# Sparse attention's position bias formed inside block 1's first feed-forward product with 128-row one-hots, and a gate unit of 48 columns that stays on the chip

## The reference

```python
gates = jax.nn.sigmoid(g.reshape(bsz, t_len, NSA_HEADS, 3))      # g: the last 48 columns of proj = h @ w_in
def nsa_mixer(q, k_cmp, v_cmp, k_slc, v_slc, k_swa, v_swa, gates, cmp_pos, cmp_w1, cmp_w2, rel_bias):
    kc = compress(k_cmp, 0); vc = compress(v_cmp, 1)              # 15 compressed keys and values
    # head_bias(dist) = tab[t5_bucket(dist)], tab = rel_bias, 32 buckets x 16 heads
    s_c = q @ kc * scale + head_bias(dist_c)                      # compressed branch
    s_s = q @ ks * scale + bias_s                                 # selected branch, the same table
    s_w = q @ kw * scale + head_bias(dist_w)                      # window branch, the same table
    return gb[..., 0:1] * o_c + gb[..., 1:2] * o_s + gb[..., 2:3] * o_w
```

## Time and profile before

| what | value |
|---|---|
| runs, median of 3 | 3845.78 us (3845.76 to 3848.34) |
| profiled execution, span | 3849.2 us |
| TensorE busy with products, weight loads | 97%, 91% of the span |
| VectorE, ScalarE, GpSimd busy | 49%, 15%, 36% |
| mean granted clock of TensorE | 0.986 of 2.4 GHz |
| bias products, gate unit, compression, nv 0 | 2619.71 to 2670.5 us of the span |

### The profile page before, as it was taken

How to read it: one execution, slowest core, us unless ns; L and a number is a source line. 1 busy time by engine, 2 the same in 40 slices (tenths; PEclk the granted TensorE clock), 3 DMA queues, 4 the chain that set the end, 5 groups by cost and what they waited for, 6 DMA issues and landing times.

```text
span 3849.2 us, 67389 instructions
## 1 busy us (share of the span) xinstructions
PE 3729.7 (97%) x29050; PEld 3506.3 (91%) x29050; DVE 1886.3 (49%) x3284; ACT 590.1 (15%) x1321; POOL 1380.1 (36%) x799
## 2 busy tenths in 40 slices
PE   9999999999999999999999999999898999999997
PEld 7888888889989999999999998878696899999997
DVE  2444426572334623111125547471633788888655
ACT  0333311111110111000000000131602211111001
POOL 0000000045546774777760000000350677775000
PEclk9999999999999999999999999999999999999999
DMA  6565665456664553444444554436342344444452
GB/s 258 196 231 211 219 238 189 175 181 225 209 206 173 222 187 144 160 169 176 165 159 162 173 203 164 169 121 171 125 165 109 133 159 172 176 162 162 163 177 84
DMA packets 124442, 677.61 MB, mean 176 GB/s; under 512 B 32208, under 2 KB 38608, under 8 KB 93808
## 3 DMA queue, kind: packets, MB, share of 16 engines
q1 hardware_dynamic: 88784, 584.37, 42.5%
q0 software_dynamic: 11824, 43.00, 3.8%
q10 hardware_dynamic: 23536, 45.92, 3.3%
HBM read 619.99 MB, written 53.25 MB: 175 GB/s over the span
## 4 chain that ended last, share of the span: by engine, by line
PE 91%; DVE 4%; ACT 1%; DVEq 1%; issue 1%; DMA 0%; ACTq 0%; SPq 0%; POOL 0%
PE product_bank L583 56%; PE product_bank L644 25%; PE product_bank L411 2%; PE product_bank L889 1%; PE mixer_bank L1587 0%; PE mixer_bank L1601 0%; PE mixer_bank L1418 0%; DVE arena L1449 0%; PE mixer_bank L800 0%; DVE yT L1446 0%; DVE yT L1161 0%; PE mixer_bank L2644 0%; PE mixer_bank L1410 0%; PE mixer_bank L2678 0%; ACT xT L1116 0%
## 5 line engine op out<-in xcount | busy, mean ns | idle before, releaser
L644 PE MATMUL product_bank<-hT,weight_ring 128*128 128x256 f32 x2752 | 608.6, 380 | 2.5 <-ACT out_stage L683 1.7
L644 PEld LDWEIGHTS product_bank<-hT,weight_ring 128*128 128x128 f32 x2752 | 522.1, 191 | 76.0 <-issue 4.5
L583 PE MATMUL product_bank<-hT,weight_ring 128*128 128x128 f32 x4128 | 518.7, 277 | 12.4 <-DVE out_stage L624 8.4
L583 PEld LDWEIGHTS product_bank<-hT,weight_ring 128*128 128x128 f32 x4128 | 490.0, 193 | 16.8 <-DVE out_stage L624 9.0
L583 PE MATMUL product_bank<-arena,weight_ring 128*128 128x128 f32 x3360 | 419.7, 275 | 1.4 <-DVE hT L624 1.4
L583 PEld LDWEIGHTS product_bank<-arena,weight_ring 128*128 128x128 f32 x3360 | 397.1, 192 | 3.6 <-DVE hT L624 1.6
L618 DVE TENSOR_TENSOR arena<-product_bank,arena 128x128 f32<-128x128 f32 x125 | 36.3, 291 | 640.7 <-PE product_bank L583 639.8
L550 POOL TENSOR_TENSOR arena<-weight_ring 128x1024 f32<-128x1024 f32 x87 | 207.1, 2380 | 353.0 <-PE product_bank L583 277.7
L553 POOL TENSOR_TENSOR weight_ring<-weight_ring 128x1024 f32<-128x1024 f32 (+1 forms) x155 | 331.2, 2137 | 0.0
L3111 DVE SCALAR_TENSOR_TENSOR arena<-arena 128x256 f32<-128x256 f32 x176 | 322.2, 1869 | 14.4 <-ACT arena L3076 11.1
L583 PE MATMUL product_bank<-xT,weight_ring 128*128 128x128 f32 x2144 | 273.9, 277 | 10.4 <-ACT xT L1116 10.4
(11 more groups left out here) (580 smaller groups left out, 5317.4 us busy)
## 6 DMA issues: line engine op xcount, KB each, us to landing
weight_ring<-in_weights SPq DMA_DIRECT2D x212, 2048.0 KB, 8.0
weight_ring<-in_weights SPq DMA_DIRECT2D x132, 512.0 KB, 5.7
weight_ring<-in_weights SPq DMA_DIRECT2D x64, 384.0 KB, 5.7
units<-out_stage ACTq DMA_DIRECT2D x87, 256.0 KB, 7.8
rwkv_keep<-arena ACTq DMA_DIRECT2D x16, 1282.0 KB, 6.1
arena<-units POOLq DMA_DIRECT2D x47, 256.0 KB, 4.5
arena<-rwkv_keep SPq DMA_DIRECT2D x8, 1280.0 KB, 12.0
arena<-units SPq DMA_DIRECT2D x27, 256.0 KB, 8.6
```

Source lines behind the costliest of these rows:

```text
L583: mm = pe.matmul(bank[:, at * P:at * P + P], lhs[:, j, :], rhs[:, j, :], start=g == 0 and n in (0, 3) and j == 0, stop=g == n_groups - 1 a ...
L644: mm = pe.matmul(psg[b][:, half * T:half * T + T], lhs, rhs, start=k == 0, stop=k == 15)
```

## The change

- The bias products move from `nsa_pe` into `ffn_pe`, behind unit 4 of 44 (`BIAS_AT`). VectorE first spreads the table into a block diagonal (`tab_spread`, after its unit 2), so that the 30 products on 32 rows become 8 on 128 rows with 64 columns (the last one 64 rows and 32 columns); the L2637 product stays. VectorE takes them out of PSUM after its unit 5, and adds the compressed mask there.
- The bias rows go to DRAM once (behind GpSimd's unit 8) and are then copied 128 times within DRAM in four parts of 4 heads (768 KB each), behind units 12, 16, 20 and 24.
- The gate unit joins the weave as quarters 57 to 60, with 48 columns instead of 256; ScalarE copies the 48 columns to SBUF, and the store and the load fall away. The sigmoid becomes the first thing after the weave. `beside_mixers` skips every fourth step instead of every third.
- SyncE's `nsa_loads` stands behind nv 1's slot load instead of mem_v 0's, no longer waits for nk before the compression's loads, and takes the queries ahead of nk. The values are loaded where all of it was.
- GpSimd's `nsa_pool` waits for `s5_done` before head 0's tiles instead of before `memT`.
- `n_BC`, `n_rows` and `n_g` lie where the one-hots were, in the constants.

The diff, cut to its core:

```diff
-STORED = ("rkv", "lora", "qk", "v", "gates", "mem_k", "mem_v", "sqk", "sv", "nq", "nkc", "nk", "nv", "ng")
+STORED = ("rkv", "lora", "qk", "v", "gates", "mem_k", "mem_v", "sqk", "sv", "nq", "nkc", "nk", "nv")
...
                 if n == UNIT_AT["branch_b0", 0][0] + RING - 1:
                     gate_loads(sp)
+                if n == UNIT_AT["nv", 1][0]:
+                    nsa_loads(sp)
                 if n == UNIT_AT["mem_v", 0][0]:
-                    nsa_loads(sp)
+                    nsa_value_loads(sp)
...
+        def unit_quarters(pe, name, u, src, step=8, arrives=None, cols=T):
-                        lhs, rhs = src[:, k, half * P:half * P + P], w[:, k, :]
-                    mm = pe.matmul(psg[b][:, half * T:half * T + T], lhs, rhs, start=k == 0, stop=k == 15)
+                        lhs, rhs = src[:, k, half * P:half * P + P], w[:, k, 0:cols]
+                    mm = pe.matmul(psg[b][:, half * T:half * T + cols], lhs, rhs, start=k == 0, stop=k == 15)
...
+                if u == BIAS_AT:
+                    bias_pe(pe)
...
+                if u >= BIAS_AT + 4 and (u - BIAS_AT) % 4 == 0 and u <= BIAS_AT + 4 + 4 * BIAS_PARTS:
+                    bias_rows_pool(pool, (u - BIAS_AT) // 4 - 1)
...
+                if u == BIAS_AT - 2:
+                    tab_spread_dve(dve)
+                if u == BIAS_AT + 1:
+                    bias_dve(dve)
...
-        n_rows = nsa_bufs[0][0]
+        n_BC, n_rows, n_g = n_oc[:, 0:480], n_oc[:, 480:864], n_oc[:, 864:960]
...
         def nsa_loads(sp):
-            stage_stored(sp, "nk")
             sp.wait_ge(sem("s5_done"), 1)
             load = lambda d, s, name="nsa_in": sp.dma_start(d, s).then_inc(sem(name), 16)
             load(n_w1, t_in["cmp_w1"], "nsa_compress_in")
+            stage_stored(sp, "nkc")
             for j in range(2):
                 u = row_of("nkc", j)
                 for par in range(2):
                     src = u[64 * par:64 * par + 64, :].rearrange("p (g t) -> p g t", g=2)
                     load(nkcs[0:64, j, par:NG:2, 0:256], src, "nsa_compress_in")
                     load(nkcs[64:128, j, par:NG:2, 0:255], src[:, :, 1:256], "nsa_compress_in")
+            for n in range(4):
+                load(n_q[:, 512 * n:512 * n + 512], row_of("nq", n))
+            stage_stored(sp, "nk")
             for j in range(2):
                 u = row_of("nk", j)
                 for par in range(2):
                     src = u[64 * par:64 * par + 64, :].rearrange("p (g t) -> p g t", g=2)
                     for base in (0, 64):
                         load(nkd[base:base + 64, j, par:NG:2, :], src)
-            for n in range(4):
-                load(n_q[:, 512 * n:512 * n + 512], row_of("nq", n))
-            stage_stored(sp, "ng")
-            load(ng, row_of("ng", 0).rearrange("p (q n) -> p q n", q=2)[:, :, 0:48])
+
+        def nsa_value_loads(sp):
             for j in range(2):
                 unit_stored(sp, "nv", j)
-                load(n_v[:, 512 * j:512 * j + 512], row_of("nv", j), "nsa_values_in")
+                sp.dma_start(n_v[:, 512 * j:512 * j + 512], row_of("nv", j)).then_inc(sem("nsa_values_in"), 16)
+
+        BIAS_PARTS = 4
+
+        def bias_rows_pool(pool, part):
+
+            if part == 0:
+                pool.wait_ge(sem("bias_steps"), 3)
+                pool.dma_start(bias_row, n_rows[0:16, 0:384]).then_inc(sem("bias_rows_stored"), 16)
+                return
+            pool.wait_ge(sem("bias_rows_stored"), 16)
+            h = slice(4 * part - 4, 4 * part)
+            pool.dma_start(bias_rows[h, :].rearrange("h (p n) -> h p n", p=P), bias_row[h, :].unsqueeze(1).to_broadcast([4, P, 384]))\
+                .then_inc(sem("bias_rows_stored"), 16)
+
+        def bias_pe(pe):
+            pe.wait_ge(sem("nsa_consts_loaded"), ALL_CONSTS)
+            pe.wait_ge(sem("bias_steps"), 1)
+            pe.matmul(pm[0][0:16, 0:256], nc_("tab")[0:32, :], nc_("onehot_rows")[0:32, :], start=True, stop=True)
+            oc = nc_("onehot_cmp")
+            for b in range(8):
+                ends = 4 if b < 7 else 2
+                r = slice(0, 32 * ends)
+                mm = pe.matmul(pm[1][:, 64 * b:64 * b + 16 * ends], oc[r, b * P:b * P + P], nc_("tab_spread")[r, 0:16 * ends],
+                               start=True, stop=True)
+            mm.then_inc(sem("bias_steps"), 1)
+
+        def tab_spread_dve(dve):
+            dve.wait_ge(sem("nsa_consts_loaded"), ALL_CONSTS)
+            for n in range(4):
+                rows = slice(32 * n, 32 * n + 32)
+                dve.tensor_copy(nc_("tab_spread")[rows, 16 * n:16 * n + 16], nc_("tab")[rows, :])
+            dve.drain().then_inc(sem("bias_steps"), 1)
+
+        def bias_dve(dve):
+            dve.wait_ge(sem("bias_steps"), 2)
+            dve.memset(n_rows[0:16, 256:384], NEG)
+            dve.tensor_scalar(n_rows[0:16, 0:256], pm[0][0:16, 0:256], 1 / HSCALE, None, ALU.mult)
+            dve.tensor_scalar(nBC, pm[1][:, 0:480].rearrange("p (q n h) -> p q h n", q=2, h=NH), 1 / HSCALE, None, ALU.mult)
+            dve.drain().then_inc(sem("bias_steps"), 1)
+            cadd = nc_("cmp_add").rearrange("p (q n) -> p q n", q=2)
+            dve.tensor_tensor(nBC, nBC, cadd.unsqueeze(2).to_broadcast([P, 2, NH, NCMP]), ALU.add)
+            dve.drain()
 
         def nsa_pool(pool):
-            pool.wait_ge(sem("bias_rows_ready"), 1)
-
-            pool.dma_start(bias_rows.rearrange("h (p n) -> h p n", p=P), n_rows[0:16, 0:384].unsqueeze(1).to_broadcast([16, P, 384]))\
-                .then_inc(sem("bias_rows_stored"), 16)
-            pool.wait_ge(sem("bias_rows_stored"), 16)
+            pool.wait_ge(sem("bias_rows_stored"), 16 * BIAS_PARTS + 16)
+            pool.wait_ge(sem("s5_done"), 1)
             for h in range(NH):
                 if h == 2:
-                    pool.wait_ge(sem("s5_done"), 1)
                     pool.dma_start(yT[:, :, :], t_in["memT"]).then_inc(sem("mem_loaded"), 16)
                 if h >= 2:
                     pool.wait_ge(sem("nsa_biased"), 2 * (h - 1))
@@ -2627,25 +2677,10 @@
                 pool.dma_start(nbias[:, h % 2, 256:384], diag).then_inc(sem(f"nsa_bias{h % 2}"), 16)
 
         ALL_CONSTS = 16 * (2 + P // N_BUCKETS)
-        N_LOADS, N_COMPRESS = 16 * (4 + 8 + 1), 16 * (1 + 8)
+        N_LOADS, N_COMPRESS = 16 * (4 + 8), 16 * (1 + 8)
 
         def nsa_pe(pe):
...
-            pe.wait_ge(sem("nsa_consts_loaded"), ALL_CONSTS)
             pe.wait_ge(sem("attn_head_done"), SB_AT + SB_HEADS)
-
-            tab = nc_("tab")[0:32, :]
-            pe.matmul(pm[0][0:16, 0:256], tab, nc_("onehot_rows")[0:32, :], start=True, stop=True)
-            oc = nc_("onehot_cmp")
-            for rows in range(4):
-                if rows:
-                    pe.drain()
-                for u in range(rows, 2 * NCMP, 4):
-                    r = slice(32 * rows, 32 * rows + 32)
-                    mm = pe.matmul(pm[1][:, u * 16:u * 16 + 16], oc[r, u // 4 * P:u // 4 * P + P], nc_("tab")[r, :],
-                                   start=True, stop=True)
-            mm.then_inc(sem("compress_steps"), 1)
-
-            run(unit_quarters(pe, "ng", 0, xT))
...
+        def nsa_gates_kept(act):
+            yield
+            yield
+            yield
+            pos, seq, _ = UNIT_AT["ng", 0]
+            act.wait_ge(w_used, pos + 1)
+            act.activation(ng, psg[seq % 4][:, :].rearrange("p (q n) -> p q n", q=2)[:, :, 0:48], ACT.Copy)\
+                .then_inc(bank_free[seq % 4], 1)
+            yield
+
         def nsa_act(act):
-            store_unit(act, "ng", 0)
-            act.wait_ge(sem("compress_steps"), 2)
+            act.drain()
+            act.activation(ng, ng, ACT.Sigmoid).then_inc(sem("nsa_gates"), 1)
+            act.wait_ge(sem("compress_steps"), 1)
...
-            act.wait_ge(sem("nsa_in"), N_LOADS)
-            act.activation(ng, ng, ACT.Sigmoid).then_inc(sem("nsa_gates"), 1)
...
-            dve.wait_ge(sem("compress_steps"), 1)
             dve.wait_ge(sem("attn_head_done"), SB_AT + SB_HEADS)
-
-            dve.memset(n_rows[0:16, 256:384], NEG)
-            dve.tensor_scalar(n_rows[0:16, 0:256], pm[0][0:16, 0:256], 1 / HSCALE, None, ALU.mult)
-            dve.tensor_scalar(nBC, pm[1][:, 0:480].rearrange("p (q n h) -> p q h n", q=2, h=NH), 1 / HSCALE, None, ALU.mult)
-            dve.drain().then_inc(sem("bias_rows_ready"), 1)
-            dve.wait_ge(sem("bias_rows_stored"), 16)
             dve.wait_ge(sem("nsa_gates"), 1)
-
-
-            cadd = nc_("cmp_add").rearrange("p (q n) -> p q n", q=2)
             cmul = nc_("cmp_mul").rearrange("p (q n) -> p q n", q=2)
-            dve.tensor_tensor(nBC, nBC, cadd.unsqueeze(2).to_broadcast([P, 2, NH, NCMP]), ALU.add)
...
-            return 2 if n < 14 else int(n % 3 > 0)
+            return 2 if n < 14 else int(n % 4 > 0)
...
-            weave(chain(*(quarters(pe, name, xT) for name in SECOND)), beside_s5(s5_pe(pe), sb_pe(pe)), beside_mixers)
```

(21 more changed lines are left out.)

## The result

| | before | after |
|---|---|---|
| median of the runs, us | 3847.1 (3845.8 to 3851.3) | 3880.2 (3878.4 to 3882.0) |
| span of the profiled execution, us | 3849.2 | 3876.6 |
| ratio to before | 1 | 1.0083 [1.0071, 1.0095] |

The account below looks back on a forecast made before the run. TensorE, busy 97% of the span, was taken to bound the kernel. -28.46 + 6.1 + 4.1 + 7.2 + 2.65 + 2.5 - 1.6 = -7.5 us off the median 3845.8 gave 3838.3 us, range 3821 to 3843.

Parts of the forecast that it names:

- Bias rows in four parts: ffn_in: GpSimd issues the bias-row DMAs in its idle time; cost 0 unless the weights come late.
- third rival: ffn_in: the bias-row parts starve the weight stream, +29 us, 3867 us in all; chance 7%.
- bias products in `ffn_in`: The bias products cost TensorE 2.5 us in their new place, bounds 2.0 and 4.0.
- longer up to the last scores: Weave: 12.3 us more work, partly filling waits, so TensorE reaches the last scores 6.1 us later; bounds 5 and 9.
- last scores to second product: Behind the last scores: 6.74 us of plain waiting with no quarter there, as long as before, so 0.
- second product to compression: Second product, three gate quarters and output at the low clock: 15.4 us against 11.30, +4.1.
- compression: The compression runs at the low clock: 15.5 us against 8.34, +7.2; bounds 14.5 to 16.7.
- nv 0 pays the clock: Unit nv 0 pays what the gate unit paid until the clock rose, +2.65 us.
- from the sparse scores to the end: Start of the heads: both chains that came late start earlier, -1.6 us, bounds 0 and -3.2.
- removed: Behind the weave: bias products (12.00 us) and gate unit (16.46) leave TensorE's path, -28.46.
- second rival: The clock rises in the middle of the compression, nothing falls on nv 0: 3832 us; chance 13%.
- Rival 1: The clock rises during the gate quarters, so the compression stays at 8.34 us: 3824.4 us; chance 28%.

Follow-up runs that it names:

- e1: The changed kernel with GpSimd's weight sum in ffn_in ordered by a counter instead of drains, transfers still on GpSimd's queue: 3835.4 us.
- e5: The changed kernel, drains and GpSimd's queue kept, each part being 32 copies of all 16 rows instead of 128 copies of 4: 3836.0 us.
- e3: The changed kernel with the bias rows in eight parts of two rows instead of four of four, on GpSimd's queue: 3921.6 us.
- e2: The changed kernel with the bias-row transfers issued from ScalarE's queue, behind a unit's sigmoid product, instead of GpSimd's: 3836.5 us.
- e11: e7 with 48 instead of 256 columns in the gate unit, nothing else changed: 3837.9 us.
- e7: e2 with the gate unit back behind the weave, 256 columns, old weave pattern: 3833.3 us. Run 7's stretch: weave's first product to first behind nv 0.
- e6: e2 with the gate unit computed with all 256 columns instead of 48, in the same place: 3833.2 us.
- e8: e2 with the gate unit ahead of the nk units and two quarters between the last scores and their second product: 3839.3 us.
- e9: e6 with one quarter left out early in the weave and two put between the last scores and their second product: 3839.3 us.

## Why the prediction was wrong

The step that failed is "Bias rows in four parts". It set the cost to 0 on two rows: GpSimd idles 2.86 us a unit, and the one big transfer kept its queue 1.05 us. The 1.05 us is the length of the instruction; behind it on GpSimd come one addition and then a drain. The step named "the next unit's weight sum" as what is queued behind the parts, and did not look into it: `sum_weights` drains between its additions, and a drain there lasts until GpSimd's own transfer has landed (e1, e5). The Trainium skill, "Perfetto Trace Analysis", section "DMA Instruction — SWDGE (GPSIMD)", says that such a row ends when the descriptors are made, not when the data have moved; the trace agrees, 1.17 us beside a landing of 16.2. The right term, worked out from after: 16.4 us from the issue to the second addition, less the 5.3 us until the first addition is done, is 11.1 of GpSimd; less the 2.6 us of lead that it has, 8.5 of TensorE; four times, with the low clock behind each, some 42 us of the 43.

The third rival had the parts slow by confinement to four engines, which is borne out (e3, e5), and an outcome near the measured one, which was luck. Its mechanism was wrong: it let the weights starve, from twice 7.7 us a slot; beside a part they landed after 11.2 to 11.5, inside the 25 us until they are needed, and TensorE waited for GpSimd's sums alone.

Point by point, for the rest, from after's own trace; the ends of each stretch are the same instructions as in the forecast:

| term | forecast | measured |
|---|---|---|
| bias products in `ffn_in` | +2.5 | +2.6 (1532.67 to 1535.24) |
| longer up to the last scores | +6.1 | +5.3 (259.26 against 253.96) |
| last scores to second product | 0 | 0.0 (7.59 in both) |
| second product to compression | +4.1 | +2.8 (14.12 against 11.30) |
| compression | +7.2 | +5.4 (13.74 against 8.34) |
| nv 0 pays the clock | +2.65 | +1.4 (15.12 against 13.75) |
| from the sparse scores to the end | -1.6 | -3.0 (1161.1 against 1164.1) |
| removed | -28.46 | -28.46 |
| sum | -7.5 | -14.0 |
| parts of the bias rows | 0 | +43 |

The sum with the last row, +29, is what the two spans differ by within 2 us (3876.6 - 3849.2 = 27.4). The 2 us lie ahead of the weave: its first product starts at 2346.86 in before and at 2346.6 to 2348.2 in the runs without the stall, so of the +2.6 for the bias products at most half arrives there; why was not looked for. Each term has its right sign, and the mechanism behind them, a clock that stays low from the 6.67 us wait until 256-column products, was right as put. The terms of the weave and of the clock were too dear and the heads' gain too small, 6.5 us in all. The bounds named in the prediction, added up, give 3834 to 3845.5 and not the 3835 to 3843 stated; it makes no difference here. With the transfers mended, e1, e2 and e5 stand 11 to 13 us below before, between the forecast and its second rival, whose mechanism (a rise within the compression) no run showed. Rival 1, a rise under the gate quarters, is refuted by after's 0.50 and by e11.

What the forecast could have said and didn't: by its own terms the gate unit's half came to -16.46 + 6.1 + 4.1 + 7.2 + 2.65 = +3.6, a loss. e7 agrees: 3833.3 without it, 3836.5 with it, and 3.0 us in the stretch of the traces named in run 7.

The fastest kernels here are e6 and e7, 3833.2 and 3833.3, 0.4% below before; they can't be told apart. Both have 256-column products ahead of the compression and no large transfer under a drain.

## What to carry to other kernels

Before a transfer is put on a compute engine's queue, read the instructions that follow it there: its cost is not the issue time but, if a drain follows, its landing. Here the landing went by the rows of the outermost dimension, and by the weights that came in beside it. Costs of narrow products are to be summed together with what runs behind them: a unit with a fifth of the columns saved 2.2 us and cost the next two 7.5. A wait that is filled with work from elsewhere must be followed to the next wait of the same chain, and the copies that the moved work leaves on another engine must be followed too: in e8 and e9 a copy on ScalarE came to stand ahead of the softmax that the chain needed.

## What was not expected of the hardware

- GpSimd's drain waited for a DRAM-to-DRAM transfer that touches nothing the additions use: 11.1 us at a landing of 16.2, 16.3 at 21.0, 0.2 at 4.1. A wait on a counter in its place cost nothing that shows (the second addition starts 0.08 us after the first ends).
- Half the bytes in half the rows landed no earlier (15.7 against 16.1 us), the same bytes in sixteen rows four times as early (4.1).
- Products of 48 columns that start at the full level ended at 1.2 GHz, with no wait of over 0.7 us in the 9 us ahead of them, and took some 0.22 us a record then, nearly what 256 columns take at the full clock (13.99 / 64 = 0.219).
